# Expert weights in fewer and longer transfers, low parts moved to VectorE in the gating stage, final norm inside the last feed-forward

## The reference, cut to what matters

```python
# experts: 16 of them, 32 tokens each, hidden width 1536
h  = silu(xg @ w_e_gate[e]) * (xg @ w_e_up[e])         # w_e_gate, w_e_up: 1024 x 1536
yo = (h @ w_e_down[e]) * gate                          # w_e_down: 1536 x 1024
# gating (gMLP), chunks of 128 tokens, 8 groups of 128 columns
u, v = split(gelu(rms_norm(x, a_norm) @ a_w_in))       # a_w_in: 1024 x 2048
v = layer_norm(v) * v_gain                             # over the 1024 columns
z = einsum('gts,bcsgd->bctgd', w_sp * causal, v) + b_sp
x = x + (u * z) @ a_w_out
# end
x = x + (silu(g) * up) @ ffn_w_down
out = x * rsqrt(mean(x*x) + eps) * final_norm
```

## Time and profile before

| What | Value |
|---|---|
| median of three runs | 1555.95 us |
| the profiled execution: its own time | 1553.9 us |
| its span, first to last instruction | 1552.1 us |
| PE busy | 1343.7 us (87%) |
| mean granted TensorE clock | 0.937 |
| DMA traffic | 446.83 MB, mean 288 GB/s |
| gate and up matmuls of the experts (line 1488), idle before them | 82.9 us, most of it until a DMA |
| down matmuls (line 1509), first of a part, idle before them | 55.9 us, most of it until a DMA |
| low parts on POOL (line 1991), mean | 4648 ns, against 2331 ns on DVE |

### The profile page before, as it was taken

One profiled execution on the slowest core, in us unless ns is written; L12 is line 12 of the kernel. 1 busy time (PEld: TensorE's weight loads), 2 busy tenths in 40 slices (PEclk: granted clock), 3 DMA queues, 4 the chain that ended last, 5 costly groups with the idle time before them and its releaser, 6 DMA issues. The chain is left out here.

```text
span 1552.1 us, 17920 instructions
## 1 busy us (share of the span) xinstructions
PE 1343.7 (87%) x7120; PEld 853.9 (55%) x7120; DVE 518.9 (33%) x878; ACT 482.3 (31%) x737; POOL 216.6 (14%) x132
## 2 busy tenths in 40 slices
PE   7999999998777776667776777999999999999998
PEld 7778878633222221222222222877888777788886
DVE  5897768310000000000000000645333436653333
ACT  6656564310000000000000000635444467564442
POOL 0010000000000000000000000761322171113221
PEclk9999999999888888888889888999999999999999
DMA  7564437999999999999999999845555454265640
GB/s 247 171 183 117 115 128 290 388 423 431 430 432 432 434 429 433 430 429 432 432 431 433 433 429 421 311 144 187 193 181 197 145 201 138 96 213 169 202 161 28
DMA packets 117793, 446.83 MB, mean 288 GB/s; under 512 B 8552, under 2 KB 61160, under 8 KB 98544
## 3 DMA queue, kind: packets, MB, share of 16 engines
q1 hardware_dynamic: 116112, 445.29, 74.0%
q10 hardware_dynamic: 1632, 0.88, 0.2%
HBM read 445.10 MB, written 1.05 MB: 287 GB/s over the span
## 5 line engine op out<-in xcount | busy, mean ns | idle before, releaser
L1488 PE MATMUL ps<-sb_ring,sb_consts 128*32 128x384 f32 x1776 | 193.9, 595 | 82.9 <-DMA sb_ring<-w_e_up 45.7
L170 PE MATMUL ps<-net_whi,sb_xhi 128*128 128x512 f32 x480 | 190.6, 397 | 1.5 <-DVE sb_xlo L2433 1.0
L172 PE MATMUL ps<-net_whi,sb_xlo 128*128 128x512 f32 x480 | 187.6, 391 | 0.0
L171 PE MATMUL ps<-net_wlo,sb_xhi 128*128 128x512 f32 x480 | 187.5, 391 | 0.0
L1509 PE MATMUL ps<-sb_e_ring,sb_hT 128*32 128x512 f32 x540 | 180.7, 649 | 2.3 <-DMA sb_e_ring<-w_e_down 2.2
L1488 PEld LDWEIGHTS ps<-sb_ring,sb_consts 128*32 128x32 f32 x1776 | 63.3, 130 | 213.6 <-issue 108.9
L1509 PE MATMUL ps<-sb_mid,sb_hT 128*32 128x512 f32 x180 | 107.0, 758 | 55.9 <-DMA sb_e_ring<-w_e_down 55.1
L1978 ACT ACTIVATE net_whi<-sb_ring 128x2048 fp32r<-128x2048 f32 x64 | 122.1, 1916 | 58.4 <-PE ps L172 55.4
L1589 DVE TENSOR_TENSOR sb_sg<-ps,sb_sg 128x384 f32<-128x384 f32 x16 | 8.9, 558 | 358.5 <-PE ps L1488 358.5
L1991 DVE TENSOR_TENSOR net_wlo<-sb_ring,net_whi 128x2048 fp32r<-128x2048 f32 x46 | 107.1, 2331 | 58.2 <-ACT net_whi L1978 58.2
L1991 POOL TENSOR_TENSOR net_wlo<-sb_ring,net_whi 128x2048 fp32r<-128x2048 f32 x18 | 83.7, 4648 | 215.7 <-ACT net_whi L1978 215.7
(11 more groups left out here) (368 smaller groups left out, 1947.6 us busy)
## 6 DMA issues: line engine op xcount, KB each, us to landing
sb_ring<-w_e_gate SPq DMA_DIRECT2D x28, 3072.0 KB, 39.1
sb_e_ring<-w_e_down SPq DMA_DIRECT2D x46, 1536.0 KB, 35.2
sb_ring<-ffn_w_gu SPq DMA_DIRECT2D x88, 512.0 KB, 4.5
sb_ring<-w_e_up SPq DMA_DIRECT2D x14, 3072.0 KB, 38.9
sb_ring<-w_e_up SPq DMA_DIRECT2D x20, 1536.0 KB, 40.7
sb_mid<-w_e_up SPq DMA_DIRECT2D x16, 1536.0 KB, 42.0
sb_mid<-w_e_down SPq DMA_DIRECT2D x15, 1536.0 KB, 32.4
sb_ring<-ffn_w_down SPq DMA_DIRECT2D x22, 1024.0 KB, 4.8
```

Of the source, the lines that this page charges most:

```text
L170: pe.matmul(out, hi, whi, start=start, stop=False)
L171: pe.matmul(out, hi, wlo, start=False, stop=False)
L172: return pe.matmul(out, lo, whi, start=False, stop=stop)
L1488: mm = pe.matmul(ps[j * CAP:(j + 1) * CAP, GATE if i < 4 else UP, 0:FJ], xgs[:, k, :], rows[:, q * E_FF + j * FJ:q * E_FF + (j + 1) * FJ], ...
```

## The change

**Expert down rows.** They are dealt so that partition p holds the 12 rows 12p to 12p+11, one run of 48 KB in memory: `load_down` takes the first 12 KB in one DMA and the other 36 KB in a second, instead of four DMAs of 12 KB. Row o belongs to group j = o % 4 and block b = o // 4. So that h comes out in that order, the gate and up columns of group j are now every fourth column (`rows.rearrange("p (q n j) -> p q j n")`), and the moving operand of line 1488 is read with a step of four numbers, 16 bytes, instead of side by side. Up units 6 and 7 now lie next to each other (`HOME`) and are loaded as a pair as well. In the last expert they stay single, and its down rows come in runs of 12, 20 and 16 KB instead of 8 and 4 KB. For expert 0 the first down part is loaded ahead of up units 6 and 7.

**Gating.** The low parts of u0 and u1 go from POOL to DVE, and the spatial product stands ahead of u1.

**End.** The final norm moves into the last feed-forward. Each half of a token tile is squared on ACT and multiplied with the gain on DVE as soon as its sum is there. DVE and ACT then scale one half each, and SP and ACT store 2 KB runs.

```diff
@@ Stream of expert loads, experts(), SP
-            def load_gate_up(e):
-                for i in PAIRS:
+            def load_pairs(e, pairs):
+                for i in pairs:
                     sp.wait_ge(used, e * NS + (i + 2 - NS))
                     load_pair(sp, m, I, e, i)
-                for i in range(len(PAIRS) * 2, NGU):
-                    load(e, i)
...
             with sp.Fori(2, LAST) as e:
-                load_gate_up(e)
+                load_pairs(e, PAIRS)
                 for i in range(NGU, NS):
                     load(e, i)
-            load_gate_up(LAST)
+            load_pairs(LAST, PAIRS[0:3])
+            sp.wait_ge(used, LAST * NS + (NGU + 1 - NS))
+            for i in range(NGU - 2, NGU):
+                load_expert(sp, m, I, LAST, i, i)
@@ constants and loaders
-PAIRS = (0, 2, 4)
+PAIRS = (0, 2, 4, 6)
+HOME = {NGU - 2: NGU - 1, NGU - 1: NGU, NGU: NGU - 2}
+def load_down(sp, m, I, e, i):
+
+    src = I["w_e_down"][0, e, :, :].rearrange("(p o) n -> p (o n)", p=P)
+    if i == 0:
+        sp.dma_start(expert_unit(m, HOME[NGU]), src[:, 0:SLOT]).then_inc(m.e_landed[NGU], 16)
+    else:
+        sp.dma_start(m.e_ring[:, 0:3 * SLOT], src[:, SLOT:]).then_inc(m.e_landed[NGU + 1], 16)
-def load_group(sp, m, I, e, j):
-
-    src = I["w_e_down"][0, e, :, :].rearrange("(j p b) n -> p j (b n)", b=FB, p=P)[:, j, :]
-    sp.dma_start(expert_unit(m, NGU + j), src).then_inc(m.e_landed[NGU + j // JP], 16)
@@ experts(), PE
                     for q in range(GK):
                         k = (i % 4) * GK + q
                         for j in range(J):
                             mm = pe.matmul(ps[j * CAP:(j + 1) * CAP, GATE if i < 4 else UP, 0:FJ], xgs[:, k, :],
-                                           rows[:, q * E_FF + j * FJ:q * E_FF + (j + 1) * FJ],
+                                           rows[:, q, j, :],
                                            start=k == 0, stop=k == DC - 1)
...
-                for i in range(NGU, NS):
-                    pe.wait_ge(landed[i], e * (16 * JP) + 16 * JP)
+                for i, rows in ((NGU, range(0, FB)), (NGU + 1, range(FB, J * FB))):
+                    pe.wait_ge(landed[i], e * 16 + 16)
                     for h in range(2):
-                        for b in range(FB):
-                            for q in range(JP):
-                                j = (i - NGU) * JP + q
...
+                        for o in rows:
+                            b, j = o // J, o % J
+                            mm = pe.matmul(ps[j * CAP:(j + 1) * CAP, DOWN[h], :], hT[:, b, j * CAP:(j + 1) * CAP],
+                                           down_rows(m, o)[:, h * BANK:(h + 1) * BANK], start=b == 0, stop=b == FB - 1)
@@ gmlp(), VectorE
                 for t in range(T):
                     ins = dve.bn_stats(bst[:, t, i, :], vt[:, t, i * BANK:(i + 1) * BANK])
+                if i == 0:
+                    for g in at["u0"]:
+                        st.split_lo(dve, g)
             link(ins)
             for t in range(T):
                 ins = dve.bn_aggr(bmv[:, t, :], bst[:, t, :, :].rearrange("p i s -> p (i s)"))
             ins.then_inc(var_ready, 1)
+            st.split_lo(dve, at["u1"][0])
             dve.wait_ge(rs_ready, 2)
             for t in range(T):
                 dve.tensor_scalar(vt[:, t, :], vt[:, t, :], bmv[:, t, 0:1], brs[:, t:t + 1], ALU.subtract,
                                   ALU.mult).then_inc(v_ready, 1)
+            st.split_lo(dve, at["u1"][1])
@@ gmlp(), PE
+                if name == "u1":
+                    spatial()
@@ swiglu(), VectorE, last feed-forward only
                     dve.tensor_tensor(dst, ps[:, ACC[2 * t + h], :], dst, ALU.add).then_inc(x_ready, 1)
+                    if final:
+                        if t == 0 and h == 0:
+                            dve.wait_ge(gain_in, 16)
+                        dve.wait_ge(x_ready, 2 * t + h + 1)
+                        dve.tensor_tensor(y[:, t, h * BANK:(h + 1) * BANK], dst, gain_row[:, h * BANK:(h + 1) * BANK],
+                                          ALU.mult).then_inc(scaled, 1)
+                        if h == 1:
+                            dve.wait_ge(first_done, t + 1)
+                            dve.wait_ge(half_sum, 2 * t + 2)
+                            dve.tensor_tensor(ends[:, t, 0:1], halves[:, t, 0:1], halves[:, t, 1:2], ALU.add).then_inc(mean_done, 1)
+                        if t == 1:
+                            dve.wait_ge(scaled, 2 * h + 1)
+                            dve.wait_ge(end_ready, h + 1)
+                            dve.tensor_scalar(y[:, h, 0:BANK], y[:, h, 0:BANK], ends[:, h, 1:2], None, ALU.mult).then_inc(y_dve, 1)
@@ swiglu(), ACT
+                for t in range(T):
+                    for h in range(2):
+                        act.wait_ge(x_ready, 2 * t + h + 1)
+                        act.activation(m.xs[:, t, h * BANK:(h + 1) * BANK], m.x[:, t, h * BANK:(h + 1) * BANK], ACT.Square,
+                                       scale=float(D) ** -0.5, accum_out=halves[:, t, h:h + 1]).then_inc(half_sum, 1)
+                    act.wait_ge(scaled, 2 * t + 2)
+                    act.wait_ge(end_ready, t + 1)
+                    act.activation(y[:, t, BANK:], y[:, t, BANK:], ACT.Copy, scale=ends[:, t, 1:2]).then_inc(y_act, 1)
```

More of the change, by code:

```diff
@@ L558, in _ @@
                     load_expert(sp, m, I, 0, 0)
-            for i in range(1, EARLY):
+            for i in range(1, RING + 2):
                 if i == RING:
@@ L1481, in hidden @@
                 for i in range(NGU):
-                    rows = expert_unit(m, i if i else first)
-                    if i - 1 not in pairs:
+                    alone = len(pairs) == 3 and i >= NGU - 2
+                    rows = expert_unit(m, first if i == 0 else i if alone else HOME.get(i, i))
+                    rows = rows.rearrange("p (q n j) -> p q j n", q=GK, j=J)
+                    if alone and i == NGU - 1:
+                        pe.wait_ge(landed[i], 3 * 16)
+                    elif i - 1 not in pairs:
                         pe.wait_ge(landed[i], e * 16 + 16)
@@ L1537, in _ @@
                 out(e)
-            hidden(LAST, pairs=PAIRS)
+            hidden(LAST, pairs=PAIRS[0:3])
         @block.vector
@@ L1785, in _ @@
             norm_pool(pool, m, use)
[L1786 to L1794 removed]
+            pool.wait_ge(var_ready, 1)
+            pool.tensor_scalar(bvar[:, :], bmv[:, :, 1], EPS, None, ALU.add).then_inc(rs_ready, 1)
+            pool.wait_ge(rs_ready, 1)
+            pool.tensor_tensor(brs[:, :], bvar[:, :], m.half[:, 0:T], ALU.pow).then_inc(rs_ready, 1)
+            for g in range(at["go0"][0], last + 2):
+                st.split_lo(pool, g)
         @block.tensor
@@ L1830, in _, with spatial @@
                         mm.then_inc(m.xturn_ps, 1)
+            def spatial():
+                pe.wait_ge(v_ready, T)
+                pe.wait_ge(wsp_ready, 1)
+                for q in range(G_GROUPS):
+                    mm = pe.matmul(ps[:, 4 + q // 2, (q % 2) * SEQ:(q % 2 + 1) * SEQ], wsp[:, q, :],
+                                   vt[:, :, q * P:(q + 1) * P], start=True, stop=True)
+                    if q % 2:
+                        mm.then_inc(sp_ps, 1)
             def turn(half):
@@ L1854, in _ @@
                                       None, part)
-                    if name == "u1" and j == 0:
-                        pe.wait_ge(v_ready, T)
-                        pe.wait_ge(wsp_ready, 1)
-                        for q in range(G_GROUPS):
-                            mm = pe.matmul(ps[:, 4 + q // 2, (q % 2) * SEQ:(q % 2 + 1) * SEQ], wsp[:, q, :],
-                                           vt[:, :, q * P:(q + 1) * P], start=True, stop=True)
-                            if q % 2:
-                                mm.then_inc(sp_ps, 1)
             for h in range(2):
@@ L1931, in _, with swiglu @@
                 add_to_x(dve, m, st, at, f"go{h}", [4 + 2 * h + t for t in range(T)], h)
-def swiglu(nc, m, I, st, at, l, use, final=False):
+def swiglu(nc, m, I, st, at, l, use, out=None):
     with ExitStack() as ctx:
@@ L1953, in swiglu @@
                              "sums_ready", "x_ready"))
+        final = out is not None
+        if final:
+            gain_row, gain_in = sb("gain_row", [P, D]), sem("gain_in")
+            y, halves, ends = sb("y", [P, T, D]), sb("halves", [P, T, 2]), sb("ends", [P, T, 2])
+            half_sum, scaled, first_done, mean_done, end_ready, y_act, y_dve = (
+                sem(s) for s in ("half_sum", "scaled", "first_done", "mean_done", "end_ready", "y_act", "y_dve"))
+            dram = out[0].rearrange("(t p) d -> p t d", p=P)
         g0 = at[f"ffn{l}"]
@@ L2085, in _ @@
             if final:
-                norm_pool_tile(pool, m, use + 1, 0)
+                for t in range(T):
+                    pool.wait_ge(half_sum, 2 * t + 1)
```

(3 more changed lines are left out.)

100 lines of the change are left out of this document (34 added, 66 removed).

## The result

| | time, us | ratio to before (95% interval) |
|---|---|---|
| before | 1555.95 (median of 11) | |
| the change | 1560.58 (median of 11, 1558.82 to 1561.68) | 1.0027 (1.0018 to 1.0037) |

A forecast was written before the change was run, and what follows sets the result against it. The prediction took DMA weight transfers to bound the experts and PE most of the rest; savings of 3.7 + 0 + 3.8 + 0.3 = 7.8 us gave 1548.0 us, with an 8-in-10 range of 1544.5 to 1557.5.

The forecast's parts named there:

- Term B: Gate and up matmuls, line 1488: reading the moving operand with a step of four numbers costs PE nothing, 0 us.
- ACT's row: Profile evidence on operand steps: ACT at 32 bytes takes 2137 ns against 1.06 us contiguous, 2.03 times.
- second rival: Experts' gate and up: the operand's step costs PE 2.03 times, the start loses 9.1 us; 1557.2 us, chance 0.17.
- the place: Experts' start: buffer room that PE must free before SP issues the next load, at 348.60 us before the change.
- The cover: Experts' start: slack before the stream loses time, 0.2 us plus 1.9 from expert 0's shorter down product.
- Term A: Expert weight transfers: longer runs shorten an expert from 43.75 to 43.53 us, 3.7 us saved in all.
- The bound from below: Lower limit for the transfers' gain: down rows keep their pace whatever the run, only the up pair gains, 0.5 us.
- my other bound: Upper limit for the transfers' gain: a fixed cost for each run, 0.30 us an expert, 5.0 us in all.
- Term C: Gating: low parts on DVE remove PE's 1.99 us wait and the slower clock after it, 3.8 us saved.
- Term D: End of the kernel: final norm by halves within the last feed-forward, 0.3 us saved, bounds -1.0 and 1.0.
- a step of 3 times: Third rival, experts 0 and 1: the operand's step costs PE 3 times; 11.9 us slower, about 1568 us, chance 0.08.

The follow-up runs named there:

- micro: Separate small program, TensorE alone with operands in place, moving columns read at different steps: 0.323 us at step 1, 0.341 at 2, 0.514 at 3, 0.680 at 4.
- after_side: The changed kernel with gate and up columns read side by side instead of with a step of four numbers (output not the reference's): 1549.45 us, ratio 0.9964.
- no_deal: The kernel before with the change's gating and end, without its expert loads, deal of down rows or step: 1551.80 us, ratio 0.9975.

## Why the prediction was wrong

**Term B failed**, "I take no loss, B = 0". The step costs 2.1 times, 0.68 us where 0.32 were, and with it 11.1 us. The row I went by, PE's loads of weights at 12 bytes, says nothing of the moving side: at 12 bytes that side costs 1.6 times (micro), and the loads' 1.4 times was already a sign that I explained away. "Which leaves room to fetch slower" was an argument from no row at all; the pace of 0.83 ns a column has room for a step of two numbers, not of four. ACT's row, 2.03 times, came nearest, and it was the row at the larger distance; that the same thing slows both engines no run shows.

**The second rival's mechanism is what happened**, and its price for the start, 9.1 us, is what the traces show (9.2), but that is luck: errors cancel. The work that delays the place was taken as 34 steps and is 40, since two units of expert 1 are eight steps. The 32 of expert 0 lose only 0.31 us each, since without the step of four they take 0.37 there and not 0.32, at a granted clock of 0.75 (304.2 to 310 us in after_side). So the delay is 12.8 us, not 11.2. The cover was taken as 0.2 + 1.9 = 2.1 us and is 3.7, since expert 0's down product takes 5.3 us (318.21 to 323.52 in after_side), not 6.8. The rival gave 1557.2 in place of 1560.6; of these 3.4 us, 1.4 are Term A (below) and the rest is the last expert, which it didn't count: no further stream runs behind it that could hide PE. Its 32 steps of 0.68, 22 us, begin 11.8 us after the last landing of expert 14, and the transposes, the down product and the scatter still follow; that is 1.9 us more than before, and by the experiments 1.2 to 2.7.

**Term A was too large**: 3.7 forecast, 2.35 by the medians (after_side against no_deal), of which 1.7 are firm. The step of it that failed is that the down rows are dearer in themselves, 7.31 and 7.40 for what a pair does in 7.25. What costs is the transfer, 0.043 us each, and nine become six: 0.13 an expert, not 0.22. By the line two single transfers take 7.31, as groups 0 and 1 did, and nearly as the up units did (7.29); why groups 2 and 3 read 7.40 stays open. The 0.15 between 7.25 and 7.40 was not a price. The bound from below, "the down rows keep their pace", was as wrong in its reason; my other bound, a fixed cost for each run, fits the line in kind and was too high in price.

**Term C had the right size** (3.8; 4.0 by the traces, 4.15 with D by no_deal) **and half the reason.** I wrote that nothing of POOL would lie beside DVE's rows; the four last operations still take 6.02 us. The product's new place, which the term doesn't name, is what hides them.

**Term D**: 0.3 forecast, 0.26 read from one execution each. The last sum starts 0.67 us later against the first, not 1.05. It wasn't timed by itself.

**The chances.** Slower had 0.08, and only by a step of 3 times. With 2.03 times taken for the step and the last expert counted, the forecast would have been about 1559, and the sign of the change the other one.

## What to carry to other kernels

Before a layout is changed so that a transfer gains, price what the engines then read with a step: for TensorE's moving operand 8 bytes between float32 columns were nearly free here (1.06), 12 cost 1.6 and 16 cost 2.1 times. What longer runs saved here was 43 ns for each transfer less, so count transfers, and weigh that against the work that the new layout pushes onto an engine. An engine that a stream hides in the loop is bare before the stream is full and after it ends; look at the first and the last turn by themselves.

## What the hardware showed beyond that

How far apart TensorE's moving columns lie costs by steps: in float32 nearly nothing at 8 bytes, 2.1 times at 16 and no more at 24 or 32; in fp32r already 1.9 times at 8 bytes (micro). The Trainium skill (SBUF — State Buffer, "Door 1: The DMA port swizzle") has lines of 16 bytes and asks for two hits on each. The float32 times agree with it, the time of fp32r at two columns to a line doesn't; nor does its figure of four float32 for how far one can stride for free. The measurement decides.

The mean granted clock rose with the slower reading: 0.937 before, 0.972 after, 0.930 in after_side. Between 500 and 600 us PE is busy for 71 of 100 us at 0.85 before, for 86 at 0.95 after, and for 63 at 0.83 in after_side: PE busy longer beside the stream rests less.
